# Loads, first modulation section and router of a two-layer hybrid decoder kernel

## The reference, cut to what matters

```python
mod = silu(c) @ ada_w[l] + ada_b[l]            # 1024 x 6144; six parts of 1024
sh1, sc1, gt1, sh2, sc2, gt2 = jnp.split(mod, 6, axis=-1)
h = modulate(rmsnorm(x, norm_mix[l]), sh1, sc1)
proj = h @ w_in[l]                             # HGRN2, latent, differential, window attention, gates
...
x = x + gt1[:, None, :] * (merged @ w_out[l])
h2 = modulate(rmsnorm(x, norm_ffn[l]), sh2, sc2)
x = x + gt2[:, None, :] * moe(h2, ...)         # 16 experts, 4 groups, top 2, router shared by the layers
```

## Time and profile before

| | us |
|---|---|
| median of 3 runs | 2452.93 (2451.09 to 2459.91) |
| the profiled execution | 2452.13 |
| its span | 2450.4 |
| TensorE matmul busy | 2293.7 (94%) |
| VectorE busy | 1418.0 (58%) |
| ScalarE busy | 1001.0 (41%) |

### The profile page before, as it was taken

The page is one execution under the profiler, slowest core; times in us unless marked ns, Lnnn a source line. Parts: engine busy times, 40 slices in busy tenths (PEclk is TensorE's granted clock), DMA queues, the critical chain, the costliest instruction groups (busy, mean ns, idle before and its releaser), DMA issues.

```text
span 2450.4 us, 32750 instructions
## 1 busy us (share of the span) xinstructions
PE 2293.7 (94%) x12032; PEld 1726.6 (70%) x12032; DVE 1418.0 (58%) x2677; ACT 1001.0 (41%) x1869; POOL 341.5 (14%) x333
## 2 busy tenths in 40 slices
PE   5999989899899999999989999989998999999997
PEld 2897777777675466777658977877866744677775
DVE  4637765645654634666556377667275455366664
ACT  2523333434453122666334333345344422246662
POOL 1002200000000210344200021000000022014440
PEclk9999999899999999999989999999999999999999
DMA  7322232231316553666462222321322284526652
GB/s 250 106 82 74 75 108 87 61 95 54 91 59 219 196 216 124 252 244 243 141 227 86 81 77 91 105 86 31 108 78 62 73 302 148 223 103 247 243 193 109
DMA packets 202109, 333.70 MB, mean 136 GB/s; under 512 B 31201, under 2 KB 162145, under 8 KB 185697
## 3 DMA queue, kind: packets, MB, share of 16 engines
q1 hardware_dynamic: 179024, 305.32, 36.8%
q0 software_dynamic: 19296, 19.98, 2.6%
q10 hardware_dynamic: 3632, 6.31, 0.7%
HBM read 352.48 MB, written 51.38 MB: 165 GB/s over the span
## 4 chain that ended last, share of the span: by engine, by line
PE 79%; DVE 9%; ACT 5%; issue 3%; DMA 3%; SPq 1%; ACTq 0%; POOL 0%; POOLq 0%; DVEq 0%
PE ps L760 74%; PE ps L758 5%; DMA ring<-in_w_in 1%; DVE ssq L1977 1%; DVE ring_rounded L1865 1%; DVE nmax L2034 1%; SPq L584 1%; ACT WH_rounded L1424 1%; DVE X L2445 1%; DMA Y<-y_rows 1%; ACT SC L1533 1%; DVE ps L2031 1%; DVE spare L1847 0%; DVE DQK L1979 0%; DMA bias_row<-in_router_bias 0%
## 5 line engine op out<-in xcount | busy, mean ns | idle before, releaser
L760 PE MATMUL ps<-H_rounded,WH_rounded 128*128 128x512 f32 x768 | 308.9, 402 | 0.0
L760 PE MATMUL ps<-X_rounded,WH_rounded 128*128 128x512 f32 x640 | 288.8, 451 | 13.2 <-ACT CM L1473 6.5
L1865 DVE TENSOR_TENSOR ring_rounded<-ring,WH_rounded 128x512 fp32r<-128x512 f32 (+2 forms) x168 | 195.2, 1171 | 175.4 <-ACT WH_rounded L1424 175.1
L760 PE MATMUL ps<-WH_rounded,X_rounded 128*128 128x256 f32 (+1 forms) x960 | 279.0, 291 | 16.5 <-issue 15.5
L760 PE MATMUL ps<-ring_rounded,X_rounded 128*128 128x256 f32 (+1 forms) x960 | 276.1, 288 | 0.0
L760 PE MATMUL ps<-WH_rounded,H_rounded 128*128 128x256 f32 (+1 forms) x960 | 275.8, 287 | 0.0
L760 PE MATMUL ps<-X_rounded,ring_rounded 128*128 128x512 f32 x640 | 253.5, 396 | 0.0
L760 PE MATMUL ps<-Y,ring 128*128 128x512 f32 x512 | 221.2, 593 | 1.9 <-ACT Y L1522 1.9
L1424 ACT ACTIVATE WH_rounded<-ring 128x512 fp32r<-128x512 f32 (+2 forms) x168 | 163.5, 984 | 139.6 <-PE ps L760 68.8
L2709 POOL TENSOR_TENSOR M<-M,SC 128x512 f32<-128x512 f32 x48 | 63.0, 1313 | 1092.5 <-DVE SC L2375 1092.5
L760 PEld LDWEIGHTS ps<-WH_rounded,X_rounded 128*128 128x128 f32 x960 | 189.5, 197 | 20.2 <-issue 18.6
(11 more groups left out here) (373 smaller groups left out, 4481.1 us busy)
## 6 DMA issues: line engine op xcount, KB each, us to landing
ring<-in_w_in SPq DMA_DIRECT2D x272, 256.0 KB, 4.0
ring<-in_ada_w SPq DMA_DIRECT2D x128, 256.0 KB, 5.2
Y<-in_moe_w_down SPq DMA_DIRECT2D x18, 1024.0 KB, 6.6
ring<-in_w_branch SPq DMA_DIRECT2D x64, 256.0 KB, 5.2
ring<-in_moe_w_down SPq DMA_DIRECT2D x14, 1024.0 KB, 5.5
gate_logits<-CM SPq DMA_DIRECT2D x44, 256.0 KB, 2.9
TM<-in_moe_w_gate SPq DMA_DIRECT2D x10, 1024.0 KB, 4.9
TM<-in_moe_w_up SPq DMA_DIRECT2D x10, 1024.0 KB, 7.3
```

The source lines that it names most:

```text
L760: ins = nc.tensor.matmul(o, lhsT, rhs, start=start, stop=stop)
L1865: ins = v.tensor_tensor(low[j][:, at:at + size], ring[:, j, at:at + size], high[i][:, at:at + size].bitcast(F32), ALU.subtract)
```

## The change

Four parts. (1) The scale1 pieces leave the ring: `row_load` loads each with one DMA into the tiles `TM` and `DQK`, which are free at that time, with a semaphore of their own, `row_loaded`; `RING_ORDER` has four `ada` pieces first instead of eight. In layer 0 SP issues x, four row loads, four ring pieces, `rw`, and then the parameters; `rw` counts on `seteven_loaded`, whose waiters (ScalarE before Silu, VectorE before its setup) want 96 instead of 80. (2) TensorE runs all four `mod_part` before the loop of layers, once Silu is done; for layer 1 two of them stand before the turns of Y and two between them, in place of fillers. VectorE runs both `ada` pairs before Y. For layer 1, SP issues three ring pieces, the parameters, the row loads and the last ring piece, all before Y. ScalarE's copies of `mod_row` stand before its Ln; `row_section` uses bank 0, `section` bank 1. (3) At the start TensorE turns x once `ident_ready` has come, and ScalarE copies it to `X`. (4) Router: the table of the sigmoid is loaded behind the shifts; the ranks are sums of `sel` shifted by whole tiles (64, 48, 32 and 16 columns wide); the two searches are one matmul per piece; the filler before it is 13 instead of 19.

```diff
-RING_ORDER = ([("ada", n) for n in range(8)] + ...
+RING_ORDER = ([("ada", n) for n in range(RING)] + ...
@@ SP
-            eng.dma_start(rw[:, :, :], a["router_w"]...).then_inc(inputs_loaded, ...)
+            def row_load(l, i):
+                w = layer("ada_w", l).rearrange("(k p) n -> p k n", p=P)
+                eng.dma_start(heads(late_ada[i], NC), w[:, :, bass.ds(D + i * 256, 256)]).then_inc(
+                    row_loaded[i // 2], p.gives(row_loaded[i // 2], 16))
...
+            for i in range(RING):
+                row_load(0, i)
+            for i in range(RING):
+                ada_load(0, ("ada", i))
+            eng.dma_start(rw[:, :, :], a["router_w"]...).then_inc(seteven_loaded, ...)
+            params(0)
...
+                    done_at = p.so_far(expert_used) - len(RELEASES) + 1
+                    for i in range(RING - 1):
+                        eng.wait_ge(expert_used, done_at + last_use(...))
+                        ada_load(l + 1, ("ada", i))
+                    params(l + 1)
+                    for i in range(RING):
+                        eng.wait_ge(expert_used, done_at + last_use((3, 4, 6, 7)[i]))
+                        row_load(l + 1, i)
+                    i = RING - 1
+                    ...
+                    ada_load(l + 1, ("ada", i))
@@ TensorE
+            for n in range(4):
+                mod_part(n)
             for l in range(DEPTH):
...
                 if l == 0:
                     warm(4, 5)
-                    for n in range(2):
-                        mod_part(0, n)
                 for c in range(NC):
                     square_sum(c)
-                for n in range(2 if l == 0 else 1, 4):
-                    mod_part(l, n)
                 warm(3, 5)
                 section(1, 1)
-                row_section(1)
+                row_section(0)
...
-                for t in range(NT):
-                    mm(ps[:, 0, t * NE:(t + 1) * NE], tri[:, :], sel[:, t], True, t == 0)
-                    for u in range(t):
-                        mm(ps[:, 0, t * NE:(t + 1) * NE], ones[:, :], sel[:, u], False, u == t - 1)
+                mm(ps[:, 0, 0:NT * NE], tri[:, :], flat(sel), True, False)
+                for d in range(1, NT):
+                    mm(ps[:, 0, d * NE:NT * NE], ones[:, :], flat(sel[:, 0:NT - d]), False, d == NT - 1)
...
-                warm(19, 5)
+                warm(13, 5)
...
-                for f in range(2):
-                    for n in range(2 * NT):
-                        ins = mm(ps[:, 1, f * BLOCKS:(f + 1) * BLOCKS], onehot[:, n], where[f][:, n], ...)
+                for n in range(2 * NT):
+                    ins = mm(bank3(1, 2, BLOCKS), onehot[:, n], where_both[:, :, n], ...)
...
-                    mod_part(l + 1, 0)
+                    mod_part(0)
+                    mod_part(1)
                 for t in range(NT):
-                    warm((13 if l + 1 < DEPTH else 20, 2, 2, 2)[t], 2)
+                    warm(((20, 2, 2, 2), (6, 0, 0, 0))[l + 1 < DEPTH][t], 2)
+                    if l + 1 < DEPTH and t:
+                        mod_part(*((2, range(NC)), (3, range(4)), (3, range(4, NC)))[t - 1])
@@ ScalarE
+            for c in range(NC):
+                b = 2 + c % 2
+                eng.wait_ge(filled[b], p.next(filled[b]))
+                act(X[:, c], bank(b), ACT.Copy).then_inc(emptied[b], p.gives(emptied[b]))
...
-            eng.wait_ge(seteven_loaded, p.next(seteven_loaded, 80))
+            eng.wait_ge(seteven_loaded, p.next(seteven_loaded, 96))
             act(cact[:, :], cact[:, :], ACT.Silu).then_inc(tables_ready, p.gives(tables_ready))
...
                 shift(3 * NC, Hc, h_ready)
+                nc.scalar.preload_act_table_set("sigmoid_and_others")
@@ VectorE
-                    ada(0, 0, 1)
-                ada(0, 2, 1)
+                    for u in (0, 2):
+                        ada(0, u, 1)
...
-                    ada(0, 0, 1, l=l + 1)
+                    for u in (0, 2):
+                        ada(0, u, 1, l=l + 1)
```

More of the change, by code:

```diff
@@ L265, in strewn, with last_use @@
     return at
+def last_use(slot):
+    return max(n for n, (b, m) in enumerate(RELEASES) if (3 * b + m) % SLOTS == slot)
 def build(nc, a, out, rate):
@@ L1082, in section, with mod_part @@
                         p.mark(emptied[b])
[L1084 removed]
+            def mod_part(n, ks=range(NC)):
                 half, i = divmod(n, 2)
                 b = 7 - half
[L1088 to L1090 removed]
+                w = heads(late_ada[n], NC)
+                if i == 0 and ks[0] == 0:
                     free(b)
[L1092 to L1107 removed]
+                    eng.wait_ge(row_loaded[half], p.next(row_loaded[half], 32))
+                for k in ks:
+                    last = i == 1 and k == NC - 1
+                    ins = mm(ps[0:1, b, i * 256:(i + 1) * 256], cact[:, k:k + 1], w[:, k], k == 0, k == NC - 1, last=last)
                     if last:
@@ L1110, in row_section @@
                         p.mark(emptied[b])
+            def row_section(b):
+                free(b)
+                for half in range(2):
+                    eng.wait_ge(emptied[7 - half], p.so_far(emptied[7 - half]))
+                    for m in range(4 * half, 4 * half + 4):
+                        last = m == NC - 1
+                        ins = mm(ps[:, b, m:m + 1], mod_row[:, tt(m)], ones[0:1, 0:1], last=last)
+                        if last:
+                            ins.then_inc(filled[b], p.gives(filled[b]))
+                            p.mark(emptied[b])
             def do(step, i):
@@ L1489, in feature_norm @@
                     act(SC[:, i], X[:, c], ACT.Square).then_inc(sq_ready[i], p.gives(sq_ready[i]))
+                if not ready:
+                    for i in range(2):
+                        eng.wait_ge(filled[7 - i], p.next(filled[7 - i]))
+                        act(mod_row[:, i * 512:(i + 1) * 512], ps[0:1, 7 - i, :], ACT.Copy).then_inc(
+                            emptied[7 - i], p.gives(emptied[7 - i]))
                 eng.wait_ge(filled[2], p.next(filled[2]))
@@ L1621, in _ @@
                 feature_norm()
-                for i in range(2):
-                    eng.wait_ge(filled[7 - i], p.next(filled[7 - i]))
-                    act(mod_row[:, i * 512:(i + 1) * 512], ps[0:1, 7 - i, :], ACT.Copy).then_inc(
-                        emptied[7 - i], p.gives(emptied[7 - i]))
                 eng.wait_ge(lamsum_ready, p.next(lamsum_ready))
```

87 lines of the change are left out of this document (34 added, 53 removed).

## The result

The changed kernel takes **2428.91 us** (median of 4 runs, 2425.60 to 2434.16) where the kernel before takes 2452.99 (2451.09 to 2459.91): a ratio of 0.9911, 95% interval 0.9893 to 0.9929. On another chip it was 2425.84 us (5 runs) beside 2448.69, a ratio of 0.9908. The forecast was 2431.0 us (2421 to 2443). Its profiled execution is the longest of the four, 2434.16 us with a span of 2432.4.

A forecast was written before the change was run, and what follows sets the result against it. Matmuls fill over three quarters of the chain, so only TensorE's standstills at start, routers and layer step count: 4.6 - 13.4 - 13.1 = -21.9 us from 2452.93 gives 2431.0 us, range 2421 to 2443.

The forecast's parts named there:

- Start: Layer 0 until the first `hf` matmul: `rw` queues behind 8.39 MB, so that matmul comes 4.6 us later.
- section(1, 1): Start, ahead of `row_section` and `gain`: priced at 1.9 us on TensorE.
- The low end of the range: Whole kernel: half of the best router (-16) and step (-16.5) bounds beside +3 at the start, 2421 us.
- Router: Router of each layer: table load, ranks, filler and search give 6.7 us, twice, so -13.4 us.
- third term: Router, filler between ranks and search: 26 instructions remain of 38, 12 x 0.22 = 2.6 us less.
- What I named as late next: Router, behind the search: 28 unchanged filler instructions, 9.26 us in layer 0, 7.68 in layer 1, outlasting the first gather.
- balance that either can tip: Router, before the search: data ready and filler's end both at 960.1 us; either can tip it by 1.5 us.
- Step: Layer 0 to layer 1: gain 16.8 us, less 2 and 1.7 us ahead of x, so -13.1 us (9 to 16.5).
- VectorE's second pair of `ada` pieces lies before Y and is hidden: Step to layer 1, ahead of x: the second pair was priced at no cost.
- That loads do not stay in order: Rival at the start: `rw` lands at 13 us, `gain` near 63, 2420 us; chance 0.1.
- The slower case: Rival at the start: `rw` lands 21.9 us later than forecast, at 56 us, giving 2455 us; chance 0.03.
- That the edits do not act: Router rival: another table load follows or filler stays the limit, 2 x 3 us less gain, 2437 us; chance 0.07.

The follow-up runs named there:

- The second profile of the changed kernel: The changed kernel run once more, word for word, on another chip: median 2425.84 us, span of its profiled execution 2425.8 us.

## Why the prediction was right, step by step

**Start: the sign and the mechanism right, the size too small** (+8.0 for +4.6). `rw` landed at 35.3, not 34.2 us (+1.1). The row products took 15.7 us and not 16.8 (-1.1): only part of the first ones found the lower clock. `colT` came at 52.93 (I said 52.8), the weighing ended at 68.04 (68.0). The term that was mis-sized is "`section(1, 1)`, 1.9 us": 3.54 us, as the window at 0.50 shows. I had priced it by a row in which TensorE came from filler; here it came from 5.14 us of waiting. With one more 0.6 us up to the first `hf` product and 1 us behind it, that is the 3.4 us.

**Behind the start: forecast 0, profile +1.5**, from a ring load near 328 us behind which TensorE ran a stretch of 4 us at the lower clock. The second profile of the changed kernel has +7.1 us at 120 and +3.7 us at 932, where the first has +8.0 and +9.5.

**The whole: partly luck.** The forecast of -21.9 us put everything into the stages with edits. By the first profile these gave -17.2 us and by the second -18.8 (+7.1, -6.7, -13.7 and -5.5). The median fell by 24.1. The second profile, 24.6 us below the kernel before, has the other 5.8 us in stages priced at nothing, 5.1 of them between 450 and 620 us. So the edits themselves gave some 3 to 5 us less than forecast, and stretches without an edit gave some 6 more. Whether the change brings these, by when its loads and waits fall, or they fell so by chance, stays open. The low end of the range, 2421, is lower than its own terms reach: half of the way to the best bounds beside +3 gives 2426, as I read it now, and the bounds in full 2423.

**Router: -6.7 twice was right in layer 0 and 1.5 us too much in layer 1.** By the shifts: table load -1.2 (I said -1.1), ranks -1.3 (-1.3), filler and search together -4.1 (-4.4, less 0.1). In the third term "12 x 0.22 = 2.6 us less" was mis-sized: the filler became 4.3 us shorter, 10.13 to 5.86 us, as part of the old one had run at half clock. So filler and data did not meet; TensorE waited 1.67 us, and the search started when the data said. What I named as late next, the 28 filler instructions, took the 1.5 us: 7.68 us before, 9.24 after. I had put this down as an uncertainty of 1.6 us; the run with the longer filler shows that it is the clock, and that all of it and 1.4 us more can be had back, less 0.7 us by which the search is then late. My "balance that either can tip" was judged by when data is ready; what it did to the clock, 2.9 us, was the larger side of it.

**Step: right by two errors that cancel** (-13.3 for -13.1). Y came 1.1 us later (I said 2). x was ready 5.85 us later (I said 3.7): the sentence "VectorE's second pair of `ada` pieces lies before Y and is hidden" was wrong, it waited 3.36 us for the last ring piece and held the first mix for 2.7 us; and the row products between the turns cost 4.1 us alone (my 1.7, with 4 as the bound at the lower clock). Behind x it gave 18.8 us and not 16.8: the split followed 10.1 us behind x where I had 11.9, and split to `gain` fell from 7.3 to 4.8 us as said.

**Rivals.** That loads do not stay in order is out: `rw` waited for all before it. What that rival had put in numbers, `rw` early and 2420 us, is close to what the run with the weights first measured, 2420.72, but by luck: its `gain` came at 68.18 us and not near 63, as the parameters were later than I had put them. The slower case needed a queue at 185 GB/s; it ran at 311 over the first 34 us. That the edits do not act is out by the router alone.

## What to carry to other kernels

Where one queue feeds the start, order it by who waits first: of the 20 us that this kernel still gained, 15 came from moving two calls. When a queue seems to recover, look which queue the bytes are on; a total of 400 GB/s hid that the loads the start waited for were nearly standing. Price an instruction by the state in which its engine will arrive: the same 16 small products cost 1.9 us behind filler and 3.5 us behind a wait. And filler that ends just before the data is ready was worth more to the router than the shortest filler (3.4 to 3.6 us a layer), for it kept up the clock of the work behind it. That the whole kernel gains by it was not shown: the medians differ by 1.0 us.

## What the runs showed of the hardware

- With a wait of 1.67 us ahead of the search, the filler behind it ran partly at a granted clock of 0.50 (28 instructions 9.21 us); with 0.38 us or none it did not (24 in 5.42, 28 in 6.28). A wait ahead of the search is not the only way to lose the clock: the kernel before had none there and took 9.26 and 7.68 us, and its clock had been at 0.58 from 955.3 to 959.0 us already. What brought it down there is open.
- A 2 MB store on ScalarE's queue and loads on SP's shared the 16 DMA engines very unevenly: 1.54 against 0.09 MB in 4.1 us.
- Small f32 products cost by the instruction: 16 of 46 columns 1.95 us, 32 of 23 columns 3.65; the twice as wide ones are no dearer each (0.11 to 0.12 us).
- Stretches at the lower clock made the same code differ by 5 us between executions of one kernel, and they and later loads by 11 us between kernels that differ elsewhere. The two medians of the changed kernel, on two chips, are 3 us apart (2428.91 and 2425.84), so edits worth 2 us show only in traces laid side by side.
